# Diffusion transformer block: one of six modulation blocks summed by TensorE in place of VectorE, and the order of the other five

## The chip, the cores and the metric

The kernel runs on one core of one Trainium2 chip. The metric is the device time of one execution in microseconds (us). A profile covers one execution; its span is a little shorter than the measured time of that execution.

## The reference, cut to what matters

One transformer block over 256 latent tokens and 256 context tokens, width 2048, float32 throughout. A conditioning vector `c` gives six modulation rows of 2048 columns each; the rest of the block uses them at different times.

```python
mod_l = jnp.split((silu_c @ w_mod[layer] + b_mod[layer])[:, None, :], 6, axis=-1)
n_l = modulate(rmsnorm(h_l, norm_mix_g[layer]), mod_l[0], mod_l[1])
z_l = n_l @ w_in_l                  # q, k, v, gMLP u and v, convolution a and g
...                                 # windowed attention, gMLP gating, 31-tap convolution
h_l = h_l + mod_l[2] * out_l        # out_l = concat(...) @ w_out
m_l = modulate(rmsnorm(h_l, norm_ffn_g[layer]), mod_l[3], mod_l[4])
h_l = h_l + mod_l[5] * grouped_moe(m_l, w_router, router_bias, w_gate, w_up, w_down)
```

`modulate(x, shift, scale)` is `x * (1 + scale) + shift`. The mixture of experts has 16 experts of width 1024, two per token. `w_mod` is 2048 x 12288. Its rows 0 and 1 are needed first. Row 2 is the gate of the attention half, rows 3 and 4 are shift and scale ahead of the router, and row 5 is the gate of the experts.

## The kernel before, in words

The engines run side by side with hand-placed semaphores. TensorE follows a list, `SCHEDULE`, written out by `make_schedule()`. SyncE (SP) loads weight chunks of 128 x 2048 floats (1 MB) in the order in which the list uses them, into six slots of `ring`; chunk n may be loaded when chunk n-6 has been used (`slot_free`). GpSimd (POOL) has its own DMA queue.

Stages of TensorE's list: rows 0 and 1 of the modulation with the input products A, G and Q0 (the first half of the queries); then `KV_` (keys and values of latent and context tokens), `Q1_` (second half of the queries), `V_` and `U_` (the gMLP halves), each in four chunks c = 0 to 3 of four steps `("win", g, k)`; then 16 chunks of `wout` (4 column groups g of 4 chunks c4); then the router, and the expert jobs, 24 chunks each. The eight attention heads lie between the `win` steps from the end of Q1 on: `("head", h, 0)` makes the scores, part 1 transposes the probabilities, part 2 multiplies by V. Between part 0 and part 1 of a head VectorE takes the maximum (`head_max`), ScalarE the exponentials, VectorE the division (`head_probs`, which signals `probs_done`).

Row 5 of the modulation is made by TensorE: 16 steps `("gate", k)` of one chunk each into bank M, 3 after each chunk of KV and 2 after each of the first two of Q1. Rows 2, 3 and 4 are made by VectorE in six blocks of 1024 columns, "halves" 0 to 5, in the function `sum_rows(n)`: for each of 16 row groups, m = 16 i to 16 i + 15 for block i, POOL loads 128 x 1024 floats (512 KB) of `w_half` into one of four half slots (`load_rows(m)`), and VectorE adds the rows times a scalar of `silu_c` to an accumulator:

```python
stt(total, half_slots[:, m % HALF_SLOTS, :], silu_c[:, m % KT, 0:1], total, ALU.mult, ALU.add)
```

A step `("half", i)` on TensorE adds up the 128 partitions of the finished accumulator. The accumulators are two, `halves[:, i % 2]`. POOL runs in order, and `load_rows(m)` waits for sum m-4. Ahead of the first load of block i it calls `start_half(i)`:

```python
pool.wait_ge(half_free, i + 1)      # half_free starts at 2, each ("half", i) step adds 1
pool.memset(halves[:, i % 2, :], 0.0).then_inc(half_zero, 1)
pool.wait_ge(half_zero, i + 1)
pool.dma_start(halves[0:1, i % 2, :], b_half[:, i * HALF:(i + 1) * HALF]).then_inc(bias_in, 16)
```

So block 2 (m = 32) can be loaded only after TensorE's step `("half", 0)`. That step stands right behind `("head", 4, 0)`, and `("half", 1)` right behind `("head", 7, 0)`. Blocks 2 to 5 are folded after `wout` (0,3), (1,3), (2,2) and (3,1). VectorE's program says how many sums come where. Before: 2 ahead of `head_norm(0)`; then the convolution; 5 after the centring of the convolution; 3 ahead of the convolution's variance (`csq`); 1 after `cnorm`; in the loop over heads h = 1 to 7 one between `head_max(h)` and `head_probs(h)` and then `(0, 2, 2, 5, 5, 5, 1, 5)[h]` after `head_probs(h)`; and 17, 16, 13, 7 ahead of the evacuation of the four `wout` groups. SP loads the first expert's pair into `once`, the buffer that holds the accumulators, only when all half sums and folds are done, and its queue is in order.

Of the kernel before, what the change touches and what calls it, by code (L numbers as in the profile page):

```python
# [45 lines left out]
FIRST_EXPERT = NE - 1  # L46

# [5 lines left out]
def make_schedule():  # L53
# [9 lines left out]
    for j, (k0, nk) in enumerate(BLOCKS):  # L63
# [16 lines left out]
        (KV_, 1): [("qT", 0)], (Q1_, 0): [("convsum",)], (Q1_, 1): [("kT",)], (Q1_, 2): [("convsq",)], (V_, 2): [("qT", 1)],  # L80
# [3 lines left out]
    for g in range(KV_, 7):  # L84
        for c in range(4):
            busy = (g, c) >= (Q1_, 3) and hpos < NH
            seq += [("win", g, 4 * c + i) for i in range(3)]
            if busy:
                seq.append(("head", hpos, 1))
            seq.append(("win", g, 4 * c + 3))  # L90
            if g == KV_:
                seq += [("gate", 3 * c + i) for i in range(3)]
            elif g == Q1_ and c < 2:
                seq += [("gate", 12 + 2 * c + i) for i in range(2)]
            seq += after.get((g, c), [])
            if busy:
                seq.append(("head", hpos, 2))
                hpos += 1
            if (g, c) >= (Q1_, 2) and hpos < NH:
                seq.append(("head", hpos, 0))  # L100
                if hpos in halves:
                    seq.append(("half", halves[hpos]))
# [3 lines left out]
             (2, 2): [("half", 4)], (3, 1): [("half", 5)], (3, 2): [("shift",), ("logits", 0), ("logits", 1), ("logits", 2)]}  # L106
# [25 lines left out]
CHUNK_STEPS = [s for s in SCHEDULE if s[0] in ("mod", "wout", "gate") or (s[0] == "win" and s[2] == first_row(*s[1:]))]  # L132
# [4 lines left out]
def constants():  # L137
# [18 lines left out]
        "before": p < c,  # L156
        "mask0": np.where(c <= p, 0, -BIG),
# [20 lines left out]
    for k, v in t.items():  # L178
# [7 lines left out]
              ("gm_gb", 2 * N), ("wr", KT * NE)]  # L186
# [11 lines left out]
def build(nc, x, ctx, params, consts, b_half, b_gate, w_mix0, w_mix, w_half, w_gmod, w_in, w_out, w_gate, w_up, w_down, out):  # L198
    with ExitStack() as stack:
# [131 lines left out]
        shift_done = sem("shift_done")  # L331
        gate_bias_in, gate_saved = sem("gate_bias_in"), sem("gate_saved")
# [86 lines left out]
        def _(sp):  # L419
# [4 lines left out]
            for n, (kind, *at) in enumerate(CHUNK_STEPS):  # L424
                sp.wait_ge(slot_free, n + 1)
                to = slot(n)
                if kind == "mod":
                    j, p, q = at
                    src = w_mix0[(j * 2 + p) * 2 + q] if j < 2 else w_mix[((j - 2) * 2 + p) * 4 + q]
                elif kind == "win":  # L430
                    src = w_in[at[0] * 4 + at[1] // 4]
                    if at[0] in (A_, G_, Q0_) and at[1] < 4:
                        to, src = to[:, 0:2 * N], src[:, at[1] * N:(at[1] + 2) * N]
                elif kind == "wout":
                    src = w_out[at[0] * 4 + at[1]]
                else:
                    src = w_gmod[at[0]]
                sp.dma_start(to, src).then_inc(landed[place(n)], 16)
                if n == NUMBER["win", Q0_, 12]:
                    sp.dma_start(const[:, FIRST_CONSTS:], consts[:, FIRST_CONSTS:CONST_COLS]).then_inc(table_in, 16)  # L440
            weights = (w_gate, w_up, w_down)
            for i in (5, 2, 0, 1, 3, 4, 6, 7, 8, 9, 10, 11):
# [3 lines left out]
                elif s == 8:  # L446
                    sp.wait_ge(half_free, 8)
                    sp.wait_ge(gatedT_done, 1)
                    sp.wait_ge(half_step, HALF_SLOTS + 6 * KT)
# [27 lines left out]
        def _(pool):  # L477
# [38 lines left out]
        def _(pe):  # L516
# [3 lines left out]
            for step in SCHEDULE:  # L520
# [69 lines left out]
                elif kind == "gate":  # L590
# [7 lines left out]
                    mm.then_inc(slot_free, 1)  # L598
                elif kind == "bcast":
# [49 lines left out]
                elif kind == "convsum":  # L649
                    pe.wait_ge(conv_done, 1)  # L650
                    pe.wait_ge(modcol_saved, 2 * NB)
                    pe.wait_ge(ctxT_saved, 8)
# [125 lines left out]
                elif kind == "logits":  # L778
                    g = step[1]
                    pe.wait_ge(hT_saved, g + 1)  # L780
                    pe.wait_ge(half_saved, 6)
# [236 lines left out]
        def _(act):  # L1018
# [92 lines left out]
            copy(vtok[:, 2:4], ps[:, 2:4, SEQ:N]).then_inc(v_saved, 1)  # L1111
            act.wait_ge(centred, 1)
# [65 lines left out]
            for g in range(3):  # L1178
# [10 lines left out]
                save_half(3 + g)  # L1189
# [84 lines left out]
        def _(dve):  # L1274
# [126 lines left out]
            sum_rows(2)  # L1401
# [18 lines left out]
            ts(small[:, 32:33], small[:, 63:64], 1.0, None, ALU.mult).then_inc(conv_done, 1)  # L1420

# [12 lines left out]

            dve.wait_ge(csum_done, 1)
# [21 lines left out]
            sum_rows(3)  # L1457
# [8 lines left out]
            sum_rows(1)  # L1466
            dve.wait_ge(probs_done, 1)
            for h in range(1, NH):
# [3 lines left out]
                if h == 1:  # L1472
                    head_norm(2)
# [16 lines left out]
                sum_rows((0, 2, 2, 5, 5, 5, 1, 5)[h])  # L1490
# [10 lines left out]
            for g in range(4):  # L1501
                sum_rows((17, 16, 13, 7)[g])
                if g == 0:
                    dve.wait_ge(bcast_saved, 4)
                if g == 3:

                    dve.wait_ge(half_saved, 6)
# [316 lines left out]
```

## Time and profile before

| | |
|---|---|
| Median of 3 runs | 1450.13 us (1447.05 to 1450.35) |
| The profiled execution | 1449.17 us, span 1447.4 us |
| TensorE (PE) busy | 1299.3 us, 90% |
| VectorE (DVE) busy | 423.1 us, 29% |
| ScalarE (ACT) busy | 209.1 us, 14% |
| DMA | 559.56 MB, mean 387 GB/s |
| Mean granted TensorE clock | 0.975 |

The busy share of an engine is a mean over stages with different limits. In the page's 40 slices one slice is 36.2 us, and a digit is a busy share in tenths. A float32 matmul is counted as two instructions, so x8 in a timeline row is four matmuls of the program. The timeline of an engine gives start, duration, line, operation and count, and in square brackets the idle time before and what ended it.

### The profile page before, as it was taken

To read this page: it belongs to the slowest core of one execution; us is meant where nothing else is said; L and a number is where in the kernel's file an instruction comes from. 1 tells how busy PE (TensorE), PEld (TensorE's weight loads), DVE (VectorE), ACT (ScalarE), POOL (GpSimd) and SP (SyncE) were. 2 spreads that over 40 slices of the span, in tenths; PEclk is the share of its full clock that TensorE was granted. 3 is DMA by queue.
4 is the path that set the end of the run, shared out by engine and by line. 5 is a ranking of instruction groups with operands and counts; after the bars stand their busy time and mean duration, and the time that the engine had idled before them with its cause. 6 is when DMAs were issued, how large, how long until landed. Compare 5 with 4: busy or idle time off the path is not lost.

```text
span 1447.4 us, 20580 instructions
## 1 busy us (share of the span) xinstructions
PE 1299.3 (90%) x8742; PEld 618.0 (43%) x8743; DVE 423.1 (29%) x803; ACT 209.1 (14%) x488; POOL 73.6 (5%) x138
## 2 busy tenths in 40 slices
PE   6899999999989998999999999997887887878857
PEld 4556444545445465433632543442442442333223
DVE  2002885877666340202111201021110111111112
ACT  2002101343001133100200110110110110011001
POOL 0001301121322000000000000000000000000000
PEclk9999999999999899999999999999999999999988
DMA  9999659687998899999999999999999999999996
GB/s 380 409 420 384 252 233 397 217 279 271 346 377 313 334 368 426 427 426 424 427 427 415 418 428 427 411 428 427 429 427 428 427 430 428 429 429 428 427 428 263
DMA packets 57450, 559.56 MB, mean 387 GB/s; under 512 B 6688, under 2 KB 6816, under 8 KB 20768
## 3 DMA queue, kind: packets, MB, share of 16 engines
q1 hardware_dynamic: 42768, 504.35, 83.4%
q0 software_dynamic: 14320, 52.01, 9.9%
q10 hardware_dynamic: 288, 2.10, 0.3%
q8 instruction: 60, 0.98, 0.3%
q14 instruction: 14, 0.11, 0.0%
HBM read 556.34 MB, written 2.10 MB: 386 GB/s over the span
## 4 chain that ended last, share of the span: by engine, by line
PE 52%; DMA 39%; DVE 5%; issue 2%; ACT 1%; DVEq 0%; SPq 0%; ACTq 0%
DMA ring<-w_up_dram 11%; PE ps L932 9%; DMA ring<-w_gate_dram 9%; PE ps L937 8%; PE ps L640 7%; DMA ring<-w_half_dram 6%; PE ps L899 5%; PE ps L956 4%; DMA ring<-w_down_dram 4%; DMA big<-w_up_dram 4%; PE ps L962 3%; DVE once L1311 3%; DMA ring<-w_in_dram 3%; PE ps L634 2%; PE ps L645 2%
## 5 line engine op out<-in xcount | busy, mean ns | idle before, releaser
L1680 DVE TENSOR_TENSOR big<-ps,big 128x1024 f32<-128x1024 f32 x60 | 70.7, 1220 | 306.5 <-PE ps L885 161.0
L937 PE MATMUL ps<-ring,big 128*64 128x512 f32 x560 | 132.9, 608 | 22.1 <-DMA ring<-w_up_dram 10.6
L640 PE MATMUL ps<-ring,big 128*128 128x512 f32 x320 | 148.1, 602 | 2.9 <-DMA ring<-w_in_dram 2.3
L1311 DVE SCALAR_TENSOR_TENSOR once<-ring,silu_c,once 128x1024 f32<-128x1024 f32 x96 | 123.2, 1283 | 62.9 <-DMA ring<-w_half_dram 57.2
L899 PEld LDWEIGHTS ps<-probs,big 128*128 128x128 f32 x1024 | 119.2, 191 | 44.3 <-issue 37.6
L899 PE MATMUL ps<-probs,big 128*128 128x96 f32 x1024 | 129.8, 280 | 1.9 <-DVE probs L1684 1.9
L932 PE MATMUL ps<-ring,early 128*32 128x256 f32 x1408 | 90.4, 406 | 30.8 <-DMA ring<-w_up_dram 18.3
L753 PE MATMUL ps<-ring,big 128*128 128x512 f32 x240 | 109.5, 614 | 0.0
L640 PEld LDWEIGHTS ps<-ring,big 128*128 128x128 f32 x320 | 58.4, 191 | 70.4 <-issue 64.8
L937 PEld LDWEIGHTS ps<-ring,big 128*64 128x64 f32 x560 | 36.2, 137 | 104.6 <-issue 66.9
L962 PE MATMUL ps<-ring,once 128*64 128x512 f32 x336 | 77.5, 598 | 3.4 <-DMA ring<-w_down_dram 3.4
L932 PEld LDWEIGHTS ps<-ring,early 128*32 128x32 f32 x1408 | 44.3, 115 | 76.9 <-DMA ring<-w_up_dram 22.6
L956 PE MATMUL ps<-ring,once 128*32 128x512 f32 x576 | 73.2, 602 | 0.3 <-DMA ring<-w_down_dram 0.3
L753 PEld LDWEIGHTS ps<-ring,big 128*128 128x128 f32 x240 | 46.9, 198 | 56.9 <-issue 56.9
L1216 ACT ACTIVATE big<-ps,modcol,scale_ffn 128x96 f32<-128x96 f32 x112 | 39.1, 429 | 206.1 <-PE ps L899 206.1
L1712 DVE TENSOR_TENSOR once<-ps,early 128x512 f32<-128x512 f32 x12 | 8.3, 692 | 192.3 <-PE ps L956 125.4
L498 POOL DMA_DIRECT2D ring<-w_half_dram x96 | 51.1, 532 | 256.9 <-DVE once L1311 256.9
L1216 ACT ACTIVATE early<-ps,modcol,scale_ffn 128x96 f32<-128x96 f32 x144 | 50.3, 429 | 77.7 <-PE ps L899 77.7
L634 PE MATMUL ps<-big,ring 128*128 128x256 f32 x256 | 58.5, 382 | 1.6 <-DMA ring<-w_in_dram 1.6
L937 PE MATMUL ps<-big 128*64 128x512 f32 x224 | 52.4, 600 | 7.5 <-DMA big<-w_up_dram 5.0
L634 PEld LDWEIGHTS ps<-big,ring 128*128 128x128 f32 x256 | 47.8, 190 | 12.5 <-DMA ring<-w_in_dram 4.7
L932 PE MATMUL ps<-big,early 128*32 128x256 f32 x608 | 40.4, 414 | 13.9 <-DMA big<-w_up_dram 7.9
(320 smaller groups left out, 1094.0 us busy)
## 6 DMA issues: line engine op xcount, KB each, us to landing
ring<-w_down_dram SPq DMA_DIRECT2D x48, 2048.0 KB, 23.4
ring<-w_up_dram SPq DMA_DIRECT2D x46, 2048.0 KB, 23.0
ring<-w_gate_dram SPq DMA_DIRECT2D x33, 2048.0 KB, 22.1
ring<-w_half_dram POOLq DMA_DIRECT2D x96, 512.0 KB, 5.9
big<-w_up_dram SPq DMA_DIRECT2D x18, 2048.0 KB, 22.3
ring<-w_mix_dram SPq DMA_DIRECT2D x32, 1024.0 KB, 11.0
late<-w_down_dram SPq DMA_DIRECT2D x16, 2048.0 KB, 23.7
big<-w_gate_dram SPq DMA_DIRECT2D x15, 2048.0 KB, 25.4
```

The source lines that it names most:

```text
L498: pool.dma_start(half_slots[:, m % HALF_SLOTS, :], w_half[m]).then_inc(half_in[m % HALF_SLOTS], 16)
L634: mm = pe.matmul(Z[b + q // 2][:, (q % 2) * SEQ:(q % 2 + 1) * SEQ], w[:, q * P:(q + 1) * P], nT[:, k, 0:SEQ], start=(k == 0 and q % 2 == 0 ...
L640: mm = pe.matmul(ps[:, b + t, :], nT[:, k, t * P:(t + 1) * P], w, start=(k == 0), stop=(k == KT - 1))
L753: mm = pe.matmul(ps[:, b + t, :], mixT[:, k, t * P:(t + 1) * P], w[:, i, :], start=(k == 0), stop=(k == KT - 1))
L899: mm = pe.matmul(Yb[:, i, at:at + BLK], tokens[:, t, k * P:(k + 1) * P], one_hot[:, t, :], start=(t == 0), stop=(t == TT - 1))
L932: mm = pe.matmul(out_b[0][BASE * f:BASE * (f + 1), :], rows[0][:, k, :], w[:, kk, f * 256:(f + 1) * 256], start=(k == 0), stop=(k == KT - 1))
L937: mm = pe.matmul(out_b[1][REST * f:REST * (f + 1), :], rows[1][:, k, :], w[:, kk, f * N:(f + 1) * N], start=(k == 0), stop=(k == KT - 1))
L956: mm = pe.matmul(Db[0][BASE * q:BASE * (q + 1), :], hT[0][:, (i % 2) * P + BASE * (i // 2):(i % 2) * P + BASE * (i // 2 + 1)], w[:, q * N: ...
L962: mm = pe.matmul(Db[1][REST * (q // 2):REST * (q // 2 + 1), q % 2, :], hT[1][:, (i % 4) * P + REST * (i // 4):(i % 4) * P + REST * (i // 4 ...
L1216: last = act.activation(to[:, k, :], Yb[:, k // 4, at:at + BLK], ACT.Identity, bias=modcol[:, 3, k, 0:1], scale=scale_ffn[:, k:k + 1])
L1311: stt(total, half_slots[:, m % HALF_SLOTS, :], silu_c[:, m % KT, 0:1], total, ALU.mult, ALU.add) \
L1680: tt(y, Yb[:, 2 * h:2 * h + 2, :].rearrange("p a n -> p (a n)"), y, ALU.add).then_inc(summed, 1)
```

## The change

Block 5 (the second half of row 4) leaves VectorE. TensorE makes it in eight steps `("scale", c)` of one chunk each (two row groups of 1024 columns; four matmuls per row pair side by side in bank T), two after each chunk of KV. ScalarE copies the row, a step `("scale_cols",)` of four small matmuls turns it into columns, VectorE adds the bias (`b_scale`). The gate chunks become 1 after each chunk of KV and 3 after each chunk of Q1. `convsum` moves from behind chunk 0 of Q1 to behind chunk 1. POOL issues its first four loads of `w_half` ahead of its work on the context tokens. VectorE's sums, now 80, stand elsewhere: 5 ahead of `head_norm(0)`, 3 right after the convolution, 2 and 4 around the new bias add, 4 after the centring, 3 after `cnorm`; the last entry of the loop's list is 2, and the `wout` groups have 12, 9, 6, 3. The fold of block 4 moves to `wout` (3,1), where that of block 5 was. The addition of the gate's bias (`gate_saved`) moves into the loop at h = 1.

```diff
-    after = {(KV_, 1): [("qT", 0)], (Q1_, 0): [("convsum",)], (Q1_, 1): [("kT",)], ...
+    after = {(KV_, 1): [("qT", 0)], (Q1_, 0): [("scale_cols",)], (Q1_, 1): [("kT",), ("convsum",)], ...
             if g == KV_:
-                seq += [("gate", 3 * c + i) for i in range(3)]
-            elif g == Q1_ and c < 2:
-                seq += [("gate", 12 + 2 * c + i) for i in range(2)]
+                seq += [("gate", c), ("scale", 2 * c), ("scale", 2 * c + 1)]
+            elif g == Q1_:
+                seq += [("gate", 4 + 3 * c + i) for i in range(3)]
...
-             (2, 2): [("half", 4)], (3, 1): [("half", 5)], ...
+             (3, 1): [("half", 4)], ...
...
@@ POOL @@
+            for m in range(HALF_SLOTS):
+                load_rows(m)
             for q in range(4):
...
-                load_rows(q)
+                load_rows(HALF_SLOTS + q)
...
-            for m in range(HALF_SLOTS, 6 * KT):
+            for m in range(2 * HALF_SLOTS, DVE_HALVES * KT):
...
@@ SP, ahead of the pair in `once` @@
-                    sp.wait_ge(half_free, 8)
+                    sp.wait_ge(half_free, 2 + DVE_HALVES)
...
@@ TensorE @@
+                elif kind == "scale":
+                    c = step[1]
+                    for i in range(2):
+                        for h in range(2):
+                            at = 64 * h + 32 * i
+                            mm = pe.matmul(T[at:at + 32, :], silu_c[:, 2 * c + i, :],
+                                           slot(n)[:, (2 * i + h) * N:(2 * i + h + 1) * N],
+                                           start=(c == 0), stop=(c == KT // 2 - 1))
+                    mm.then_inc(slot_free, 1)
+                elif kind == "scale_cols":
+                    pe.wait_ge(scale_row, 1)
+                    for q in range(4):
+                        mm = pe.matmul(T[:, 2 * q:2 * q + 2], modrow[:, 0, q * P:(q + 1) * P], k_("pick"),
+                                       start=True, stop=True)
+                    mm.then_inc(scale_col, 1)
                 elif kind == "convsum":
                     pe.wait_ge(conv_done, 1)
+                    pe.wait_ge(scale_added, 1)
...
@@ ScalarE @@
+            act.wait_ge(slot_free, used_chunk(NUMBER["scale", KT // 2 - 1]))
+            copy(modrow[:, 0, :], T).then_inc(scale_row, 1)
             act.wait_ge(centred, 1)
...
@@ VectorE @@
-            sum_rows(2)
+            sum_rows(5)
             head_norm(0)
...
             ts(small[:, 32:33], small[:, 63:64], 1.0, None, ALU.mult).then_inc(conv_done, 1)
+            sum_rows(3)
...
+            sum_rows(2)
+            dve.wait_ge(scale_col, 1)
+            tt(modcol[:, 4, 8:16, 0]..., T[:, 0:8]..., par("b_scale")..., ALU.add).then_inc(scale_added, 1)
+            sum_rows(4)
             dve.wait_ge(csum_done, 1)
...
-            sum_rows(5)
-            dve.wait_ge(gate_bias_in, 16)
-            dve.wait_ge(slot_free, used_chunk(NUMBER["gate", KT - 1]))
-            tt(modrow[:, 1, :], M, modrow[:, 1, :], ALU.add).then_inc(gate_saved, 1)
+            sum_rows(4)
...
-            sum_rows(3)
             dve.wait_ge(centred, 1)
...
-            sum_rows(1)
+            sum_rows(3)
             dve.wait_ge(probs_done, 1)
...
-                sum_rows((0, 2, 2, 5, 5, 5, 1, 5)[h])
+                sum_rows((0, 2, 2, 5, 5, 5, 1, 2)[h])
...
-                sum_rows((17, 16, 13, 7)[g])
+                sum_rows((12, 9, 6, 3)[g])
```

## Rows read from the trace of the kernel before

**Rows 1.** The page: the span, and TensorE and DMA in 40 slices.

```profile
span 1447.4 us, 20580 instructions
...
PE   6899999999989998999999999997887887878857
...
DMA  9999659687998899999999999999999999999996
```

**Rows 2.** TensorE's timeline: small matmuls into columns (L546), three gate chunks (L596).

```profile
120.72 0.95 PE L546 MATMUL ps<-const,modrow 128*128 128x2 f32 x8
...
165.59 2.78 PE L596 MATMUL ps<-ring,silu_c 128*32 128x512 f32 x24
```

**Rows 3.** VectorE's timeline after the convolution.

```profile
217.51 1.22 DVE L1367 TENSOR_REDUCE ss<-work 128x8 f32<-128x1024 f32 x1 [4.48 <-ACT work L1109]
```

**Rows 4.** The chain that ended last: chunk 0 of Q1 (start us, us, what).

```profile
219.13 7.07 PE ps L640 x16
```

**Rows 5.** SP's timeline: the first refill after KV.

```profile
217.48 0.33 SPq L438 DMA_DIRECT2D ring<-w_in_dram  x1
```

**Rows 6.** DMA from 233 to 250 us: bytes by queue, share of 16 engines (q1 SP, q0 POOL).

```profile
DMA packets 1325, 6.90 MB, mean 406 GB/s; under 512 B 143, under 2 KB 143, under 8 KB 824
...
q1 hardware_dynamic: 564, 4.10, 57.9%
q0 software_dynamic: 760, 2.79, 41.5%
```

**Rows 7.** TensorE's timeline at heads 4 and 5.

```profile
298.76 1.05 PE L583 MATMUL ps<-once,const 128*32 128x512 f32 x4
...
305.70 1.09 PE L699 MATMUL ps<-const,probs 128*128 128x128 f32 x8 [0.54 <-DVE probs L1454]
...
319.75 1.09 PE L699 MATMUL ps<-const,probs 128*128 128x128 f32 x8 [2.20 <-DVE probs L1454]
320.68 3.48 PE L640 MATMUL ps<-ring,big 128*128 128x512 f32 x4
```

**Rows 8.** Timelines of VectorE (head 3, first sum of block 3) and POOL.

```profile
286.56 1.22 DVE L1445 TENSOR_REDUCE small<-ps 128x2 f32<-128x1024 f32 x1
...
290.31 0.88 DVE L1454 TENSOR_SCALAR probs<-probs,small 128x512 f32<-128x512 f32 x2
...
363.75 0.97 POOL L490 MEMSET once<- 128x1024 f32 x1
...
369.72 2.67 DVE L1311 SCALAR_TENSOR_TENSOR once<-ring,silu_c,once 128x1024 f32<-128x1024 f32 x2 [1.24 <-DMA ring<-w_half_dram]
```

**Rows 9.** TensorE's timeline in the output projection.

```profile
390.77 1.84 PE L587 MATMUL ps<-const,once 128*128 128x1 f32 x16
...
399.43 1.04 PE L766 MATMUL ps<-const,big 128*128 128x128 f32 x8
...
434.46 1.97 PE L766 MATMUL ps<-const,big 128*128 128x128 f32 x8 [4.75 <-DVE big L1529]
436.22 15.92 PE L753 MATMUL ps<-ring,big 128*128 128x512 f32 x32
...
453.69 13.98 PE L753 MATMUL ps<-ring,big 128*128 128x512 f32 x32
...
476.96 2.81 PE L587 MATMUL ps<-const,once 128*128 128x1 f32 x16 [1.55 <-DVE once L1311]
479.63 9.61 PE L753 MATMUL ps<-ring,big 128*128 128x512 f32 x16
```

**Rows 10.** SP's timeline: loads for the first expert.

```profile
479.80 0.33 SPq L460 DMA_DIRECT2D once<-w_gate_dram  x1
...
524.10 5.51 SPq L460 DMA_DIRECT2D ring<-w_down_dram  x3
```

**Rows 11.** Stretches: each engine's busy time, TensorE's clock, DMA share, GB/s.

```profile
515.00:520.00 5.00, 4.70 (x42) 4.43 (x42) 3.68 (x24) 3.89 (x10) 0.00 (x0) 1.00 0.62 213
520.00:525.00 5.00, 5.00 (x76) 3.78 (x78) 2.04 (x9) 2.15 (x5) 0.00 (x0) 1.00 0.65 275
```

More of the change, by code:

```diff
@@ L46 @@
 FIRST_EXPERT = NE - 1
+DVE_HALVES = 5
 GROUPS = [("a", 2560), ("g", 3072), ("q0", 0), ("kv", 1024), ("q1", 512), ("v", 2048), ("u", 1536)]
@@ L79, in make_schedule @@
     after = {
-        (KV_, 1): [("qT", 0)], (Q1_, 0): [("convsum",)], (Q1_, 1): [("kT",)], (Q1_, 2): [("convsq",)], (V_, 2): [("qT", 1)],
+        (KV_, 1): [("qT", 0)], (Q1_, 0): [("scale_cols",)], (Q1_, 1): [("kT",), ("convsum",)], (Q1_, 2): [("convsq",)], (V_, 2): [("qT", 1)],
     }
@@ L105, in make_schedule @@
     after = {(0, 0): [("bcast", 1), ("gated",), ("bcast", 2)], (0, 1): [("bcast", 3)], (0, 3): [("half", 2)], (1, 3): [("half", 3)],
-             (2, 2): [("half", 4)], (3, 1): [("half", 5)], (3, 2): [("shift",), ("logits", 0), ("logits", 1), ("logits", 2)]}
+             (3, 1): [("half", 4)], (3, 2): [("shift",), ("logits", 0), ("logits", 1), ("logits", 2)]}
     for g in range(4):
@@ L129, in first_row @@
     return k // 2 * 2 if g in (A_, G_, Q0_) and k < 4 else k // 4 * 4
-CHUNK_STEPS = [s for s in SCHEDULE if s[0] in ("mod", "wout", "gate") or (s[0] == "win" and s[2] == first_row(*s[1:]))]
+CHUNK_STEPS = [s for s in SCHEDULE if s[0] in ("mod", "wout", "gate", "scale") or (s[0] == "win" and s[2] == first_row(*s[1:]))]
 NPRE = len(CHUNK_STEPS)
@@ L156, in constants @@
         "before": p < c,
+        "pick": (p % 32 == 0) & (p // 64 == np.arange(2)[None]),
         "mask0": np.where(c <= p, 0, -BIG),
@@ L331, in build @@
         shift_done = sem("shift_done")
+        scale_row, scale_col, scale_added = sem("scale_row"), sem("scale_col"), sem("scale_added")
         gate_bias_in, gate_saved = sem("gate_bias_in"), sem("gate_saved")
@@ L435, in _ @@
                     src = w_out[at[0] * 4 + at[1]]
+                elif kind == "scale":
+                    to = to.rearrange("p (k n) -> p k n", k=2)
+                    src = w_half[DVE_HALVES * KT + 2 * at[0]:DVE_HALVES * KT + 2 * at[0] + 2].rearrange("k p n -> p k n")
                 else:
@@ L598, in _ @@
                     mm.then_inc(slot_free, 1)
+                elif kind == "scale":
+                    c = step[1]
+                    if c == 0:
+                        pe.wait_ge(modcol_saved, 2 * NB)
+                        pe.wait_ge(ctxT_saved, 8)
+                    for i in range(2):
[11 more added lines that the diff above has]
+                    mm.then_inc(scale_col, 1)
                 elif kind == "bcast":
@@ L780, in _ @@
                     pe.wait_ge(hT_saved, g + 1)
-                    pe.wait_ge(half_saved, 6)
+                    pe.wait_ge(half_saved, DVE_HALVES)
                     for i in range(4):
@@ L1188, in _ @@
                 last.then_inc(hT_saved, 1)
-                save_half(3 + g)
+                if g != 1:
+                    save_half(3 + g // 2)
             act.wait_ge(hsq_done, 6)
@@ L1433, in _ @@
             finish_heads(N)
+            sum_rows(2)
+            dve.wait_ge(scale_col, 1)
+            tt(modcol[:, 4, 8:16, 0].rearrange("p (h q) -> p h q", h=2), T[:, 0:8].rearrange("p (q h) -> p h q", h=2),
+               par("b_scale").rearrange("p (h q) -> p h q", h=2), ALU.add).then_inc(scale_added, 1)
+            sum_rows(4)
             dve.wait_ge(csum_done, 1)
@@ L1472, in _ @@
                 if h == 1:
+                    dve.wait_ge(gate_bias_in, 16)
+                    dve.wait_ge(slot_free, used_chunk(NUMBER["gate", KT - 1]))
+                    tt(modrow[:, 1, :], M, modrow[:, 1, :], ALU.add).then_inc(gate_saved, 1)
                     head_norm(2)
@@ L1791 @@
         "wr": a["w_router"].reshape(KT, P, NE).transpose(1, 0, 2).reshape(P, -1),
+        "b_scale": columns(b_mod[4 * D + HALF:5 * D], 8),
     }
```

8 lines of the change are left out of this document (3 added, 5 removed).

## The prediction

> **What bounds the kernel now.** I read the page first [rows 1]. DMA is full from slice 14 to the end, so the end of the expert stage is when the stream of weights, once it no longer pauses, has moved its bytes. What can be won or lost lies ahead of it: when that stream gets going. There, in slices 4 to 13, DMA has pauses and TensorE is at nine tenths or more in all slices but one. So from KV to the router TensorE's own list sets the pace, plus the few places where it waits. I then read its timeline for the idle times in brackets, and each gap's releaser. Three gaps are over 1 us: 2.20 us at head 5 [rows 7], 4.75 us ahead of the transposes of the output projection and 1.55 us at the last fold [rows 9]. All three end on VectorE, which was late because of sums of `w_half`. Two things follow each gap: the wait, and a stretch in which matmuls of the same shape take up to twice as long, the lower of the clock's two levels (1.2 against 2.4 GHz).
>
> The hand-over to DMA: SP's queue waits for the last fold before it loads the first expert's pair into `once` at 479.80 [rows 10]; it is at (3,1) of `wout` before and after. The stream then pauses only between 515 and 525 us, where DMA's share is 0.62 and 0.65 [rows 11], about 3.6 us, until the first chunks of the first job are used (524.10, [rows 10]). Whatever moves TensorE's path at 524 moves the end by as much: if the fold moves 2.5 us more than that path does, the pause shrinks by 2.5 us. So I sum over TensorE's path.
>
> **Part by part.**
>
> *Block 5 on TensorE.* Three gate chunks take 2.78 us [rows 2], with the overlap about 2.71, so 0.90 a chunk. A scale chunk is the same four 32-column matmuls of 512. KV has 12 chunks of extra work before and after; Q1 has 12 gate chunks where it had 4. So +8 x 0.90 = +7.2 us. `scale_cols` has the shape of the small matmuls at 120.72: +0.9. ScalarE's copy comes just after KV, a row of 6.9 us before its use: nothing. The same goes for POOL's earlier loads and the 5 sums ahead of `head_norm(0)`: VectorE has slack behind it, as it waits 4.48 us for ScalarE after the convolution [rows 3]. The 3 sums put there take 3 x 1.3 = 4.0 us (two are 2.67, [rows 8]), so this gap covers them; without it they would delay K's rotation, which TensorE needs only 20 us later. The bias adds are small VectorE work beside TensorE.
>
> *DMA in Q1.* Q1 now eats 16 chunks instead of 8. The first refill is issued at 217.48 [rows 5] and Q1 starts at 219.13 [rows 4]. The third gate chunk of c = 2 (`gate` 12) comes after ten refills. TensorE without waits wants it after three rows (3 x 6.9), eight gate chunks (7.2), `scale_cols` (0.9) and about 2.7 for K's transposes and the convolution's sum (1.04 for eight transposes [rows 9], the rest an estimate from it, twice the columns): 219.1 + 20.7 + 7.2 + 0.9 + 2.7 = 250.6. By then the wire must have carried 10 chunks (10.5 MB) and about 9 half loads (4.7 MB), which VectorE's 2, 4 and 4 sums ask for in the same time. At 406 GB/s [rows 6] that is 15.2 MB, 37.4 us, from about 217.9: 255.3. So TensorE waits 4.7 us in Q1 where it did not wait. From below: if the half loads came last, 10.5 MB would be in at 243.7, and the wait is 0. From above: SP has moved some 2.8 MB by 227 us (9 us at 406 GB/s, less three half loads still in flight there), and if it then gets only what it got beside POOL, 4.10 MB in 17 us = 241 GB/s [rows 6], the last 7.7 MB take 32 us, to 259: 8.4. I take 4.7, and 1.7 for the clock as after the wait of 2.20 at head 5 (3.48 [rows 7] against a quarter of 7.07 [rows 4]), from 0 to 2.9: +6.4. On the shares: 760 packets of POOL carried 2.79 MB and 564 of SP 4.10 MB [rows 6], so SP had 43% of the packets. The Trainium skill (DMA: Bandwidth & Descriptors, Queues, rings and completion order) says that an engine takes turns between its queues packet by packet. By equal turns of packets of these sizes SP would get 66% of the bytes, 270 GB/s, and the upper bound would be 4.9 us instead of 8.4; the trace has it lower, and the sum goes by the byte balance.
>
> *The first sum of block 2.* This I find by counting. Sums ahead of the loop are 5+3+2+4+4+3 = 21 (they were 11); h = 1 adds 3, h = 2 adds 3, h = 3 adds one and five: 33. So the last of the five at h = 3 is m = 32, the first of block 2. Its load stands behind `start_half(2)`, which needs the step `("half", 0)`, right after `("head", 4, 0)`. VectorE must do this sum before `head_max(4)`. Before, m = 32 came at h = 5, long after. The price: `("half", 0)` is over at 299.74 (298.76 plus about 1, [rows 7]); POOL then clears the accumulator, sends the bias and loads; at block 3 the time from the start of that memset to the first sum was 369.72 - 363.75 = 5.97 [rows 8]. So the sum starts at 305.8 and ends at 307.1. From `head_max` to the end of `head_probs` takes 291.19 - 286.56 = 4.6 [rows 8]: 311.7. TensorE is ready for the probabilities of head 4 at 305.16 (305.70 less 0.54, [rows 7]). It waits 6.6 instead of 0.54: +6.1, and the clock after it as after the wait of 4.75: 1.97 against 1.04, and 15.92 against 13.98 [rows 9], +2.9. Together +9.0, from 6.5 (a shorter landing, the clock as at head 5) to 11. All of it is on TensorE's path, since nothing else is queued there. Behind the waiting VectorE stand `head_max(4)`, the exponentials, and half loads 36 on. The Trainium skill (DMA: Bandwidth & Descriptors, Anatomy of one DMA) gives 2.0 us plus bytes over 436 GB/s for a load from GpSimd, 3.2 us for 512 KB. By it the sum would start 1.1 us sooner, for the whole about 8; the row contains queueing that the page's formula leaves out.
>
> *Head 5.* Its wait (2.20) came from half loads issued too late behind five sums. After the long wait at head 4 TensorE runs slow for a while and POOL's queue has caught up, so I take it as gone: -2.2 - 1.7 = -3.9; from 0 to -3.9.
>
> *Output projection.* VectorE has 30 sums here instead of 53, and the two evacuations that TensorE waited for come on time: 12 sums are 16 us and a group of `wout` takes 28 (13.98 for two chunks, [rows 9]). The wait of 4.75 and its clock (0.9 + 1.9) go: -7.6. One fold less: -1.7 (1.84 with its overlap). At the last fold the wait of 1.55, the slow fold (2.81 against 1.84) and the slow chunk (9.61 against 6.99) go: -5.1. I price this at its full value, since no other engine is due there; if a half load still were late, up to 5 would come back.
>
> **The sum.** 7.2 + 0.9 + 6.4 + 9.0 - 3.9 - 7.6 - 1.7 - 5.1 = +5.2 us on 1449.17, so 1454.4; the median of the runs shown is 1 us over that execution. I say 1455.
>
> **Rivals.**
> 1. *The first sum of block 2 costs, Q1's DMA keeps up* (the half loads yield, or the ring was fuller than I count). 5.2 - 6.4 = -1.2: 1448. For it: DMA was full in this stretch before too, and TensorE never waited. Against: eight chunks more in some 40 us.
> 2. *Q1 waits, but the sum at head 4 is covered*, because a late DMA in Q1 or a load landing in under 4 us leaves VectorE little to wait for. 5.2 - 9.0 + 3.9 (head 5 waits as before) = +0.1: 1449. Against: the order of the two steps on TensorE leaves VectorE no way round.
> 3. *Faster: neither costs.* 5.2 - 6.4 - 9.0 + 3.9 = -6.3: 1443. The mechanism is the output projection alone: the 23 sums gone from it give 14.4 and the rest costs 8.1. The kernel is faster as long as the two new waits together cost under 6 us, and by over 0.3% if they cost under 2.
> 4. *Worse:* a second late load, at head 5 or at block 3's first sum (m = 48, between heads 7 and the gMLP product), costs a further 4 to 8: 1461.
>
> **Chances.** Forecast 0.45, its own range 1450 to 1460; rival 1 0.25; rival 2 0.08; rival 3 0.14; rival 4 0.08. The range for 8 in 10 is 1443 to 1462, between rival 3 and a little over rival 4. Within 0.3% of before (4.4 us, about what a measurement of this kernel can tell from no change) fall a third of the forecast and most of rivals 1 and 2: 0.38. Slower: the rest of the forecast, and rival 4: 0.43. Faster: 0.19.
>
> **What would show it.** In the profile after: on TensorE 12 gate chunks in Q1, and idle time there ended by `w_gmod` or `w_in` loads, some 5 us; the transposes of head 4's probabilities with an idle time of 6 to 7 us ended by VectorE, and VectorE's sum before `head_max(4)` waiting some 6 us for `w_half`; POOL's memset of block 2 released by TensorE's fold, not by VectorE; no idle time over 1 us in `wout`; the load into `once` 5 to 8 us later than 479.8. The forecast is wrong if the wait at head 4 is under 3 us, if Q1 shows none, or if DMA pauses longer between the fold and the first job.

## The result, and the profile after

The changed kernel takes 1469.18 us (median of 4 runs, 1463.52 to 1472.26), the kernel before 1450.24 us (4 runs on the same chip, 1447.05 to 1451.93). The ratio is 1.0125, with an interval of 1.0095 to 1.0155: slower by 18 to 19 us. The forecast was 1455 in a range of 1443 to 1462. The profiled execution is the fastest of the four, 1463.52 us with a span of 1461.7, so 14.3 us over the span of before.

The page after: the span, and TensorE and DMA in 40 slices, to be read beside [rows 1].

```profile
span 1461.7 us, 20651 instructions
...
PE   6999998989999997998999999998877888778866
...
DMA  9999669966796599999999999999999999999996
```

The digits hardly tell the two apart; the stretches do. TensorE's timeline after, first Q1 (beside [rows 4]), then heads 4 and 6 (beside [rows 7]), then the output projection (beside [rows 9]):

```profile
229.18 1.05 PE L622 MATMUL ps<-const,modrow 128*128 128x2 f32 x8
230.49 7.13 PE L666 MATMUL ps<-ring,big 128*128 128x512 f32 x16 [0.26 <-DMA ring<-w_in_dram]
...
241.30 1.07 PE L604 MATMUL ps<-ring,silu_c 128*32 128x512 f32 x8 [1.83 <-DMA ring<-w_gmod_dram]
...
253.84 1.06 PE L604 MATMUL ps<-ring,silu_c 128*32 128x512 f32 x8 [0.65 <-DMA ring<-w_gmod_dram]
257.62 1.06 PE L604 MATMUL ps<-ring,silu_c 128*32 128x512 f32 x8 [2.72 <-DMA ring<-w_gmod_dram]
258.62 3.63 PE L684 MATMUL ps<-once,const 128*128 128x256 f32 x8
...
328.22 1.97 PE L724 MATMUL ps<-const,probs 128*128 128x128 f32 x8 [6.46 <-DVE probs L1485]
329.98 3.62 PE L666 MATMUL ps<-ring,big 128*128 128x512 f32 x4
...
356.17 1.09 PE L724 MATMUL ps<-const,probs 128*128 128x128 f32 x8 [1.68 <-DVE probs L1485]
...
454.79 26.34 PE L778 MATMUL ps<-ring,big 128*128 128x512 f32 x61
...
488.71 1.84 PE L595 MATMUL ps<-const,once 128*128 128x1 f32 x16
490.42 7.11 PE L778 MATMUL ps<-ring,big 128*128 128x512 f32 x16
```

Up to here it is the forecast: TensorE waits 5.46 us for DMA in Q1 (the four waits down to 257.62), 6.46 us at head 4, and in `wout` the gaps of 4.75 and 1.55 us are gone, with the slow folds and chunks behind them. VectorE and POOL at head 4 (beside [rows 8]):

```profile
322.32 1.28 DVE L1339 SCALAR_TENSOR_TENSOR once<-ring,silu_c,once 128x1024 f32<-128x1024 f32 x1 [9.16 <-DMA ring<-w_half_dram]
323.53 1.22 DVE L1476 TENSOR_REDUCE small<-ps 128x2 f32<-128x1024 f32 x1
...
316.48 0.95 POOL L496 MEMSET once<- 128x1024 f32 x1 [9.83 <-PE ps L591]
```

The memset is released by TensorE's fold (L591), the sum of m = 32 starts 5.84 us after it, and `head_max(4)` stands right behind that sum. SP's timeline (beside [rows 10]):

```profile
490.59 0.33 SPq L466 DMA_DIRECT2D once<-w_gate_dram  x1
...
529.75 2.05 SPq L466 DMA_DIRECT2D ring<-w_down_dram  x2
543.34 0.34 SPq L475 DMA_DIRECT2D big<-w_gate_dram  x1
...
596.48 0.33 SPq L475 DMA_DIRECT2D big<-w_gate_dram  x1
```

The load behind the first job's first chunks is issued at 529.75, before at 524.10: TensorE's path ahead of the experts grew by 5.65 us, where the sum had 5.2. That leaves 14.3 - 5.65 = 8.6 us of the span, and these were not forecast. TensorE's timeline of before where it enters the loop over pairs of expert jobs (the two calls of `experts` with "lead" and "second"):

```profile
559.80 3.57 PE L932 MATMUL ps<-ring,early 128*32 128x256 f32 x32 [4.91 <-issue]
```

The same in the kernel after, and the start of the second and third iteration:

```profile
565.33 1.08 PE L957 MATMUL ps<-ring,early 128*32 128x256 f32 x8 [4.79 <-issue]
569.75 2.79 PE L957 MATMUL ps<-ring,early 128*32 128x256 f32 x24 [3.35 <-issue]
...
693.83 1.50 PE L957 MATMUL ps<-ring,early 128*32 128x256 f32 x24 [2.88 <-issue]
...
816.41 1.50 PE L957 MATMUL ps<-ring,early 128*32 128x256 f32 x24 [2.84 <-issue]
```

"Issue" is idle time in which TensorE waited for no semaphore that the profile shows. Both kernels have it once at the loop's entry. The changed one has it again 8 recorded matmuls into the body, in each of the three iterations. What an iteration costs is read between every second `w_gate` load into `big` on SP's queue. The stretches of two iterations before (columns as in [rows 11], the first time being the length):

```profile
587.15:707.41 120.26, 117.14 (x1028) 48.07 (x1028) 17.77 (x32) 13.66 (x38) 0.00 (x0) 1.00 1.01 425
707.41:827.64 120.23, 117.15 (x1028) 48.09 (x1028) 17.77 (x32) 13.66 (x38) 0.00 (x0) 1.00 1.00 421
```

And after, the two with such a wait in them and the one behind them, where the loop is left:

```profile
596.48:719.11 122.63, 117.28 (x1028) 47.99 (x1028) 17.76 (x32) 13.69 (x38) 0.00 (x0) 1.00 1.00 413
719.11:841.70 122.59, 117.29 (x1028) 47.99 (x1028) 17.77 (x32) 13.68 (x38) 0.00 (x0) 1.00 1.00 413
841.70:961.92 120.22, 117.14 (x1028) 48.09 (x1028) 17.76 (x32) 13.69 (x38) 0.00 (x0) 1.00 1.00 416
```

TensorE works 117.1 of 120.3 us in an iteration, so there is hardly room to hide 2.9 us. The account of the 14.3 us: 5.65 ahead of the experts; 3.7 in the first iteration, whose piece from 543.34 to 596.48 is 53.14 long and was 49.46 (537.69 to 587.15); 2.4 in each of the other two; 0.2 in what follows, as the net of small differences of both signs. The other runs of the changed kernel are up to 9 us longer than the profiled one; e2 and e3 below show one way in which such runs can differ.

These rows also bear on the prediction's first paragraph, which took a full DMA for the limit from slice 14 on. In the loop TensorE sets the pace: with the wait the share is still 1.00, but at 413 GB/s where it was 421 to 425. So a share of 1.00 does not show that DMA could move no more. Only behind 962 us does TensorE wait for weights at most chunks (1 to 3 us each, DMA at 428 GB/s from 1100 to 1300 us).

### The profile page after: what moved, and what is told of

Same layout as the page of the kernel before. It is cut to its first block, busy times and chain, and to the rows that moved or that the text cites. A ratio compares the mean times of both kernels' runs of the same rounds, so it can differ in the third digit from the quotient of the medians.

```text
span 1461.7 us, 20651 instructions
## 1 busy us (share of the span) xinstructions
PE 1299.1 (89%) x8798; PEld 616.4 (42%) x8799; DVE 402.3 (28%) x788; ACT 209.6 (14%) x488; POOL 65.6 (4%) x120
## 4 chain that ended last, share of the span: by engine, by line
PE 58%; DMA 34%; DVE 4%; issue 2%; ACT 1%; DVEq 0%; SPq 0%; POOL 0%; ACTq 0%
DMA big<-w_up_dram 14%; DMA big<-w_gate_dram 12%; PE ps L957 10%; PE ps L962 8%; PE ps L778 7%; PE ps L924 5%; PE ps L666 5%; PE ps L981 5%; PE ps L987 3%; DMA ring<-w_mix_dram 3%; DMA ring<-w_in_dram 3%; PE ps L660 2%; PE ps L671 2%; DMA ring<-w_gmod_dram 1%; PE ps L910 1%
## 5 line engine op out<-in xcount | busy, mean ns | idle before, releaser
L666 PE MATMUL ps<-ring,big 128*128 128x512 f32 x320 | 148.5, 603 | 3.1 <-DMA ring<-w_in_dram 2.5
L1339 DVE SCALAR_TENSOR_TENSOR once<-ring,silu_c,once 128x1024 f32<-128x1024 f32 x80 | 102.8, 1285 | 45.9 <-DMA ring<-w_half_dram 41.2
L778 PE MATMUL ps<-ring,big 128*128 128x512 f32 x240 | 104.7, 593 | 0.0
L504 POOL DMA_DIRECT2D ring<-w_half_dram x80 | 42.6, 534 | 217.5 <-DVE once L1339 217.5
```

The source lines that it names most:

```text
L504: pool.dma_start(half_slots[:, m % HALF_SLOTS, :], w_half[m]).then_inc(half_in[m % HALF_SLOTS], 16)
L666: mm = pe.matmul(ps[:, b + t, :], nT[:, k, t * P:(t + 1) * P], w, start=(k == 0), stop=(k == KT - 1))
L778: mm = pe.matmul(ps[:, b + t, :], mixT[:, k, t * P:(t + 1) * P], w[:, i, :], start=(k == 0), stop=(k == KT - 1))
```

## The experiments

Each is compared with the kernel before on its own chip (medians 1446 us). "First job" is the time of TensorE's first matmul for the experts in the profiled execution (before 522.10, after 527.76), "rest" the span less that time (before 925.3, after 933.9). "Q1" is the sum of TensorE's waits for DMA there (0 and 5.46), "head 4" its wait for that head's probabilities (0.54 and 6.46). The last four columns come from one profiled execution each; in e2, e3, e5 and e8 it was the slowest one.

| | median us (range, runs) | ratio, interval | first job | rest | Q1 | head 4 |
|---|---|---|---|---|---|---|
| e1 | 1455.77 (1453.60 to 1458.91, 6) | 1.0069, 1.0041 to 1.0096 | 527.52 | 926.1 | 4.37 | 6.42 |
| e8 | 1455.85 (1454.74 to 1457.83, 7) | 1.0074, 1.0050 to 1.0098 | 530.09 | 925.9 | 4.89 | 6.33 |
| e2 | 1455.28 (1453.45 to 1466.12, 6) | 1.0064, 1.0036 to 1.0092 | 520.77 | 943.4 | 0 | 0.20 |
| e3 | 1469.10 (1463.01 to 1474.99, 4) | 1.0151, 1.0109 to 1.0193 | 528.71 | 944.5 | 4.65 | 2.96 |
| e4 | 1455.50 (1453.26 to 1462.06, 8) | 1.0073, 1.0043 to 1.0103 | 519.83 | 934.5 | 4.49 | 0.20 |
| e5 | 1454.22 (1449.17 to 1460.28, 10) | 1.0056, 1.0036 to 1.0076 | 516.70 | 941.8 | 2.36 | 0 |
| e6 | 1464.22 (1461.45 to 1465.41, 4) | 1.0139, 1.0096 to 1.0182 | 523.35 | 936.3 | 0 | 6.30 |
| e7 | 1439.49 (1435.28 to 1441.97, 10) | 0.9958, 0.9939 to 0.9976 | 511.14 | 927.4 | 0 | 0 |

**e1: where the loop's code lies.** The theory: the eight `scale` steps, `scale_cols` and the fold that went add 28 matmuls net to TensorE's program (the page's PE instructions grew by 56, from 8742 to 8798, and its weight loads by as many), so some 112 instructions (the few instructions that only wait are not counted), and what follows lies that much further on. The waits are code being fetched. 36 matmuls more, in a branch that this routing never takes, move the loop by 144 further instructions. The rival: the weight stream started 11 us late, and the loop pays for that.

```diff
@@ TensorE, experts() of the changed kernel @@
+                if first and parts == (1,):
+                    for _ in range(36):
+                        pe.matmul(Z[0], ident, k_("spread"), start=True, stop=True)
```

> The changed kernel, with 36 matmuls (144 TensorE instructions) put into a branch of the first expert job that is not taken, so that nothing more is executed but the loops over expert jobs stand 144 instructions further on. With the 112 instructions that the change adds ahead of them (28 matmuls of 4) that makes 256, one fetched block of 16 KB. Theory F (code fetch: the new idle times of 2.8 to 3.4 us labelled issue, just inside the loop at 569.75, 693.83 and 816.41, come from where the loop's start lies in a fetched block): they vanish, TensorE's path from the first job to 960 us takes about 8 us less, 1458 to 1462 in the median, and the two waits ahead of the router stay. Rival D (the stream of weights starts 5 us later relative to TensorE, and the pair loop pays for it): the idle times and the time stay, 1465 to 1470.

TensorE's timeline of e1, at the loop's entry and at the start of the second iteration:

```profile
565.08 3.64 PE L960 MATMUL ps<-ring,early 128*32 128x256 f32 x32 [4.78 <-issue]
...
686.88 1.93 PE L960 MATMUL ps<-ring,early 128*32 128x256 f32 x32
```

Its stretches, as above:

```profile
592.79:713.27 120.48, 117.15 (x1028) 48.08 (x1028) 17.77 (x32) 13.68 (x38) 0.00 (x0) 1.00 1.00 424
713.27:833.49 120.22, 117.14 (x1028) 48.08 (x1028) 17.77 (x32) 13.68 (x38) 0.00 (x0) 1.00 1.01 423
```

The waits inside the loop are gone, the iterations are back at 120.2 to 120.5 us, and the span is 8.1 us below that of after at nearly the same first job (527.52 against 527.76) and the same late load into `once` (490.30 against 490.59). The rival falls: with the stream as late as in after, the rest is 926.1 us. The median is below the 1458 to 1462 that were expected, but so is that of the kernel before on this chip (1446.41, against 1450.24 beside the changed kernel), so it is the ratios that are to be compared.

**e2: the same in the kernel before.** 28 dead matmuls at the same place put its loop where the change puts it.

```diff
@@ TensorE, experts() of the kernel before @@
+                if first and parts == (1,):
+                    for _ in range(28):
+                        pe.matmul(Z[0], ident, k_("spread"), start=True, stop=True)
```

> The kernel before, with 28 matmuls (112 TensorE instructions) in the branch that is not taken, so that the loops stand where they stand in the changed kernel. Theory F: idle times of about 3 us labelled issue appear just inside the loop in three iterations, and the time rises by 6 to 10 us, to 1456 to 1460. Rival D: no change, 1450 within 3.

TensorE's timeline of e2, at the entry and in the second iteration:

```profile
558.25 1.05 PE L935 MATMUL ps<-ring,early 128*32 128x256 f32 x8 [4.70 <-issue]
562.94 2.79 PE L935 MATMUL ps<-ring,early 128*32 128x256 f32 x24 [3.64 <-issue]
...
690.33 1.74 PE L935 MATMUL ps<-ring,early 128*32 128x256 f32 x24 [3.36 <-issue]
692.00 3.73 PE L899 MATMUL ps<-probs,big 128*128 128x96 f32 x16
```

The waits come to a kernel in which nothing else is changed, again after 8 recorded matmuls, and it is 0.64% slower. In this execution, the slowest of e2's six, each wait is also followed by the low level of TensorE's clock (x16 in 3.73 us, where it takes 2.02 in the kernel before), and the stretch from one `w_gate` load to the next but one is 126.32 us. Taken over the second and third iterations of after and e2 to e6, a wait that the low level does not follow (2.83 to 3.27 us, in after, e4 and e6) makes the iteration 2.3 to 2.8 us longer, and one that it follows (3.03 to 3.62 us, in e2, e3 and e5) 3.9 to 6.2 us. The length of the wait alone does not decide: the low level came after 3.26 us in e3 and not after 3.27 in e4. That this spreads the runs of the kernels that have the wait is likely and not shown, since one execution of each was profiled and the kernel before, which has no such wait, spreads over 12 us in 22 runs.

**e8: a shorter shift.** As e1, with 12 dead matmuls, 48 instructions.

```diff
@@ TensorE, experts() of the changed kernel @@
+                if first and parts == (1,):
+                    for _ in range(12):
+                        pe.matmul(Z[0], ident, k_("spread"), start=True, stop=True)
```

> The changed kernel with 12 matmuls (48 instructions) in the branch that is not taken, instead of 36. In the changed kernel the second idle time comes 8 recorded matmuls after the loop's first, so some 24 instructions after its start a fetched block ends. If the loop is slow only because its start lies just ahead of a block's end: 48 instructions more put the start just behind that end, the second idle time vanishes as with 36, and the ratio is 1.004 to 1.010. If what counts is the distance in whole blocks from the kernel before, it stays, with 1.011 or more.

TensorE's timeline of e8 at the entry, the only such wait in the loop over pairs:

```profile
567.87 3.64 PE L960 MATMUL ps<-ring,early 128*32 128x256 f32 x32 [5.00 <-issue]
```

The rest is 925.9 us and the ratio that of e1. It is thus no matter of the amount of code, or of being back at the old place in a block (e1 is 256 instructions past before, e8 160), but of one bad place (112 past it). What distance is enough was not tried between 112 and 160. In the later loop over single jobs e8 has a wait of 3.00 us labelled issue that no other kernel has, at 1389.20. The others wait up to 2.97 us for a load of weights there, and e8's rest is no longer than e1's: where DMA sets the pace such a wait costs nothing.

**e3: the sum of m = 32 one place later.** The change's list of sums in the loop over heads, with one of the five at h = 3 moved to h = 4. The theory of the prediction, that VectorE does m = 32 ahead of `head_max(4)`, would have the wait there gone.

```diff
-                sum_rows((0, 2, 2, 5, 5, 5, 1, 2)[h])
+                sum_rows((0, 2, 2, 4, 6, 5, 1, 2)[h])
```

> The changed kernel with one number moved: the loop's list has 4 and 6 where it has 5 and 5, so that the first sum of block 2 (m = 32) comes after head_max(4) instead of ahead of it. If that sum is what TensorE waited 6.46 us for: the wait at head 4 falls under 1 us, the slow matmuls after it go (3 us), a wait of up to 4 us at head 5 comes back, and TensorE starts the first job 5 to 9 us earlier than at 527.8. If VectorE is late there for another reason (the half loads are slow): the wait stays at 4 us or more. The time falls by 5 to 9 us if the end follows the start of the first job, to 1460 to 1464.

TensorE's and VectorE's timelines of e3:

```profile
325.48 1.09 PE L724 MATMUL ps<-const,probs 128*128 128x128 f32 x8 [2.96 <-DVE probs L1485]
342.90 1.97 PE L724 MATMUL ps<-const,probs 128*128 128x128 f32 x8 [5.56 <-DVE probs L1485]
...
322.96 1.29 DVE L1339 SCALAR_TENSOR_TENSOR once<-ring,silu_c,once 128x1024 f32<-128x1024 f32 x1 [4.73 <-DMA ring<-w_half_dram]
...
337.00 1.28 DVE L1339 SCALAR_TENSOR_TENSOR once<-ring,silu_c,once 128x1024 f32<-128x1024 f32 x1 [4.82 <-DMA ring<-w_half_dram]
```

The expectation missed: I had overlooked that the loop has one sum between `head_max(h)` and `head_probs(h)`. At h = 4 that is now m = 32, still ahead of the probabilities. The wait moved by one instruction on VectorE and shrank to 2.96, and the half loads, now in a burst of one and six sums, came late at head 5 (5.56). The sum, 8.5 us, is about that of after (6.46 and 1.68, 8.1), and the first job came 0.95 us later instead of 5 to 9 sooner. For the places of the loop's fetch this run gives the same as after: TensorE's rows behind the wait of 3.53 us (the first is the wait's):

```profile
698.65 1.78 PE L957 MATMUL ps<-ring,early 128*32 128x256 f32 x24 [3.53 <-issue]
700.36 3.73 PE L924 MATMUL ps<-probs,big 128*128 128x96 f32 x16
704.01 3.17 PE L957 MATMUL ps<-big,early 128*32 128x256 f32 x32
```

**e4: fewer half loads in Q1.** Four of the eight sums around the centring go to the first `wout` group, so POOL asks for less while Q1's chunks load. By this m = 32 also becomes one of the five sums behind head 4's probabilities.

```diff
-            sum_rows(4)
+            sum_rows(2)
             dve.wait_ge(csum_done, 1)
...
-            sum_rows(4)
+            sum_rows(2)
...
-                sum_rows((12, 9, 6, 3)[g])
+                sum_rows((16, 9, 6, 3)[g])
```

> The changed kernel with two sums fewer on each side of the convolution's centring (2 and 2 where it has 4 and 4) and four more ahead of the first group of the output projection (16 for 12). That takes four half loads (2.1 MB) out of Q1, and it also moves m = 32 behind head_max(4). If the byte balance of Q1 is the cause of its 5.5 us of waits: 2.1 MB at about 410 GB/s is 5.1 us, so the waits fall to 0 to 2 us, and the wait at head 4 goes as in the run with 4 and 6. TensorE reaches the first job 10 to 13 us before 527.8. If the gate chunks alone are too many for SP's queue, the waits in Q1 stay at 4 us or more. In time: 1455 to 1460.

The first job comes 7.9 us sooner than in after (10 to 13 were expected), but not by way of Q1: the wait there is 4.49 us (5.46, 4.37, 4.89 and 4.65 in the four kernels with the old sums), where 0 to 2 was expected. What went is head 4's 6.46, for 0.20 there, 2.11 at head 5 and 2.19 at head 6 (1.68 in after). The waits of the loop stay (3.40, 3.27, 3.20).

**e5: sums spread so that no load is late at a head.** As e4, with the sums of the loop thinned out from h = 3 to 5, three fewer in all, made up for in `wout`. m = 32 falls between `head_max(5)` and `head_probs(5)`.

```diff
-                sum_rows((0, 2, 2, 5, 5, 5, 1, 2)[h])
+                sum_rows((0, 2, 2, 4, 3, 4, 2, 2)[h])
-                sum_rows((12, 9, 6, 3)[g])
+                sum_rows((16, 12, 6, 3)[g])
```

> The changed kernel with the sums spread otherwise: 2 and 2 around the centring (4 and 4), the loop's list (0, 2, 2, 4, 3, 4, 2, 2), and 16, 12, 6, 3 in the output projection. So m = 32 comes at head 5, some 12 us after the fold that frees its accumulator, and no head has more than five sums (2.6 MB in the 12 us of a head). The run with 4 and 6 left m = 32 between head_max(4) and head_probs(4), and only moved the wait on. If it is the late start of block 2 together with too many half loads in a head: the waits at heads 4 to 6 (8.1 us, and some 4 us at the lower clock) fall under 1.5 us in all, Q1's waits of 4 to 5 us stay, and the first job starts at 516 to 519. With the code where the change has put it, a ratio to before of 1.003 to 1.008. If VectorE is late for another reason, the waits stay over 4 us.

At the heads TensorE waits for 0.33 us in all, in `wout` for nothing over 0.7, and the first job starts at 516.70: 11 us sooner than in after and 5.4 sooner than before. The loop's waits (3.32, 3.53, 3.03) take all of that and more: the ratio is 1.0056. Q1 has 2.36 us here, where 4 to 5 were expected, and 4.49 in e4, with the same steps and the same sums there.

**e6: the gate chunks moved from Q1 to KV.** KV gets 4 chunks of extra work per chunk, Q1 gets 2.

```diff
-                seq += [("gate", c), ("scale", 2 * c), ("scale", 2 * c + 1)]
+                seq += [("gate", 2 * c), ("gate", 2 * c + 1), ("scale", 2 * c), ("scale", 2 * c + 1)]
             elif g == Q1_:
-                seq += [("gate", 4 + 3 * c + i) for i in range(3)]
+                seq += [("gate", 8 + 2 * c + i) for i in range(2)]
```

> The changed kernel with four more gate chunks in KV (two after each chunk instead of one) and two instead of three after each of Q1. DMA moves 240 GB/s in KV, where each chunk takes 17 us, and Q1 then has 12 chunks instead of 16. If Q1's waits (5.5 us in the profile of the change) are bytes that come too late: they fall under 1.5 us, the wait at head 4 stays at 6 to 7 us, and the first job starts at 522 to 524 instead of 527.8. If they come from the sharing with POOL's loads alone, 3 us or more stay. Ratio to before 1.008 to 1.011.

Q1 has no wait for DMA, and the first job is 4.4 us sooner, inside what was expected. Of the 5.5 us of waits that went, 3.6 came back as waits for VectorE at heads 0 and 1 (2.64 and 0.93), where it stood 2.44 us for `w_half`. Head 4 waits as in after. The time shows nothing of the 4.4 us: the ratio is 1.0139, above the 1.008 to 1.011 that were expected, and its interval contains the 1.0125 of after. The rest is 2.4 us longer than in after, and the first wait inside the loop is 4.21 us, the longest seen.

**e7: all of it.** e5 and e6, with the 36 dead matmuls of e1.

> Both of these, and the 36 matmuls in the branch that is not taken. If the three costs are separate and add: TensorE starts the first job at 511 to 515, no idle time labelled issue but the one at the first entry of the loop, and a ratio to before of 0.993 to 0.999, a version faster than both. If DMA takes the place of what is removed (it has little room left once the stream runs), the ratio is 1.000 or more.

TensorE's timeline of e7, at the end of Q1, at the fold and head 4, and at the loop's entry; then SP's:

```profile
253.73 2.00 PE L684 MATMUL ps<-once,const 128*128 128x256 f32 x8
...
308.43 1.05 PE L591 MATMUL ps<-once,const 128*32 128x512 f32 x4
...
314.67 1.04 PE L724 MATMUL ps<-const,probs 128*128 128x128 f32 x8
...
548.42 3.64 PE L960 MATMUL ps<-ring,early 128*32 128x256 f32 x32 [4.49 <-issue]
...
472.30 0.33 SPq L466 DMA_DIRECT2D once<-w_gate_dram  x1
```

None of the three waits is there. The first job starts at 511.14, as expected, and the kernel takes 0.9958 of the time before (0.9939 to 0.9976): the kernel with block 5 on TensorE is the faster one once the three costs around it are taken away. Of the 11.0 us by which the first job comes sooner than before, the span keeps 8.9 (6.4 by the medians). That block 5 itself brings this is not shown. e7 also spreads VectorE's sums anew, and the kernel before, whose waits of 2.20, 4.75 and 1.55 us all come from those sums, was not run with a better order of its own.

## Why the prediction was wrong

The sum ahead of the experts held, 5.65 against 5.2. That it is so close is in part luck: some terms erred against each other, and in two executions of the old schedule (before and e2) the first job starts 1.3 us apart.

- *Block 5 on TensorE*, forecast +7.2 and +0.9: where TensorE does not wait, two gate chunks in a row take 1.92 us in Q1 of e7 and three 2.78 in after, about 0.9 each as forecast, and `scale_cols` takes 1.05.
- *DMA in Q1*, forecast 4.7 of waits and 1.7 for the clock: 5.46, and L684 takes 3.63 where it takes 2.00 without the wait (e7). The late transfers are shown as the cause (0 in e6 and e7), and all but the wait of 0.26 are ended by `w_gmod`. My byte balance named one wait at the third gate chunk of c = 2; the wait came in four pieces, the first ahead of chunk 1. Halving the sums there took away little (e4) or half (e5), so the balance, by which four half loads fewer are worth 5.1 us, does not give the size.
- *The first sum of block 2*, forecast 6.6 and 2.9 for the clock: 6.46, and 1.97 and 3.62 behind it where 1.09 and 1.88 stand elsewhere, 2.6 together. The count of sums to m = 32 was right to the place, the load took 5.84 from the memset (5.97), and in e4, e5 and e7, where the sum comes later, the long wait is gone.
- *Head 5*, forecast gone: it is, but 1.68 us stand at head 6 instead.
- *Output projection*, forecast -7.6, -1.7 and -5.1: no wait is left in it. The wait of 4.75 is not a fixed part of the kernel before, though: e2, whose schedule is the same, has 0.63 and 2.33 us there and its first job at 520.77.
- *The load into `once`*, forecast 5 to 8 us later: 10.8. DMA stood idle in front of it, from 470 to 490 us (0.00 to 0.01; before only from 475 to 480). In return the pause that stood at 515 to 525 before [rows 11] is gone:

```profile
480.00:485.00 5.00, 5.00 (x19) 2.68 (x18) 0.83 (x1) 1.07 (x2) 0.00 (x0) 1.00 0.01 3
485.00:490.00 5.00, 5.00 (x23) 2.85 (x21) 0.00 (x0) 0.00 (x0) 0.00 (x0) 1.00 0.00 0
...
515.00:520.00 5.00, 4.36 (x28) 2.67 (x27) 3.99 (x26) 0.20 (x1) 0.00 (x0) 1.00 0.98 415
520.00:525.00 5.00, 4.71 (x42) 4.44 (x42) 3.71 (x24) 4.12 (x10) 0.00 (x0) 1.00 1.02 433
```

The step that failed is "Whatever moves TensorE's path at 524 moves the end by as much". It takes the experts' code as costing the same wherever it lies. The runs showed that the place of the loop in TensorE's program has a price of its own: 8.0 us in the profiled execution (3.4 + 2.2 + 2.4 in three iterations, after against e1), and more where the low level of the clock follows the wait. The sum had no term for it. With that price taken away the step holds: in e1 the first job is 5.4 us later than before and the span 6.2, in e8 8.0 and 8.6. That is the case the forecast describes, and there the ratio is 1.0069 and 1.0074: 9 to 10 us by the medians, where 5 were forecast and the traces have 6 and 9. The forecast 5 lies just below both intervals (5.9 and 7.2 us at their lower ends), so a few microseconds stay that no experiment accounts for. The profiled execution of before lies 3 us above that kernel's median on the chips of e1 and e8, which may be part of that. The forecast's other rivals don't help: rivals 1 to 3 fall, since both new waits came at their full size, and rival 4's later load (head 6) cost 1.7, not 4 to 8.

That the waits come from where the code lies is shown by moving it with code that never runs, in both directions (e1 and e8 against after, e2 against before). That they are fetches of code is the reading that fits this and the DMA record. The share by queue in the stretch 566 to 569 us of the kernel after, inside the wait that ends at 569.75:

```profile
q1 hardware_dynamic: 87, 1.26, 99.5%
q8 instruction: 1, 0.02, 2.3%
```

One packet of the instruction queue is moved there, beside 87 packets of weights on full engines. By itself that decides nothing, since kernels without the wait have such a packet too, 0.7 us (before, 681.75) and 1.1 us (e1, 688.0) after the start of the second iteration. What ties the two together is the time: in all three iterations of after and of e2, TensorE goes on 2.3 to 2.7 us after the packet (567.25 and 569.75, 691.50 and 693.83, 814.00 and 816.41 in after; 560.50 and 562.94, 688.00 and 690.33, 814.25 and 816.90 in e2; the packets' times to a quarter of a microsecond). So the kernels differ not in whether a block is fetched there but in how soon TensorE needs it. The Trainium skill (Runtime: NRT & Kernel Launch, Instruction fetch mechanics) says that code is fetched in blocks of 16 KiB, 256 instructions, ahead of the engine, that crossing a block's end is mostly hidden, and that a branch out of the fetched window waits for a fetch. The trace agrees on the block (one packet of 0.02 MB) and on the branch (4.5 to 5.1 us at the loop's entry in all kernels). It does not agree on the crossing right behind a branch: there 2.8 to 4.2 us were seen in each iteration of the kernels with that placement. That the block's end lies just there, behind the first 8 recorded matmuls of the body with their weight loads, is my reading of where the wait stands; no run shows the addresses.

What stays open: how far from the bad place is far enough; why Q1 waits 4.49 us in e4 and 2.36 in e5; where the last few microseconds of e1's and e8's ratio come from; whether the kernel before would gain as much from a better order of its sums; and why the kernel before waits 4.75 us in `wout` in one profiled execution and not in the other.

## What to carry to other kernels

When an edit adds or removes instructions ahead of a hot loop of an unrolled engine program, look in the trace for idle time with no semaphore behind it a few instructions into the loop's body, and try some dozens of dead instructions before judging the edit. When a block of work is moved between engines, count the items of every ordered list that it shifts: here one more sum ahead of head 4 was the first of a new block, whose buffer came free only with a step of TensorE at that head. And spread the loads of two queues by when each is needed: both new waits, in Q1 and at head 4, went by moving steps, at no cost in work.

## What the runs showed of the hardware that was not expected

- In a loop of 120 us beside a full DMA, TensorE stood idle for 2.8 to 4.2 us in each iteration where the loop's start had the bad place (after and e2 to e6), and not at all with 48 instructions of never-executed code ahead of it (e8). In the times that is a ratio to before of 1.0125 against 1.0074, some 7 us.
- The DMA share alone did not show whether DMA was the limit: it was 1.00 in iterations at 413 GB/s and 1.00 to 1.01 at 421 to 425.
- Waits of nearly one length in the loop left TensorE's granted clock at its high level in some executions (after, e4, e6, mean 1.00 over the iteration) and were followed by the low one in others (e2, e3, e5): x16 took up to 3.73 us instead of 2.02, and the iteration 124.1 to 126.5 us instead of 122.6 to 123.0.
